# The scan's small products set between the main ones over several halves, and the last projection done for one half of the columns and then for the other

## What is computed

```python
u_a, z_a, b_c, c_c, h_c, z_c, g_a, g_c = jnp.split(x @ w_in, SPLIT_POINTS, axis=-1)
y_a, hr, hi = ssm_branch(u_a, ...)   # 64 groups: complex diagonal scan of 64 states, then GELU and a GLU
y_a = (y_a * jax.nn.silu(z_a)) @ w_out_a
y_c = (b_c * conv3(c_c * h_c) * jax.nn.silu(z_c)) @ w_out_c
merged = jax.nn.sigmoid(g_a) * y_a + jax.nn.sigmoid(g_c) * y_c
r = DN_ALPHA * x + merged @ w_o
rc = r - mean(r); out = rc * rsqrt(mean(rc * rc) + eps) * ln_g + ln_b
```

## Time and profile before

| | |
|---|---|
| median of 3 runs | 1627.57 us (1622.84 to 1632.72) |
| profiled execution, its own time | 1623.52 us |
| its span | 1621.7 us |
| PE busy | 97% of the span |
| granted TensorE clock, mean | 0.976 of full |

### The profile page before, as it was taken

How to read it: one execution, slowest core, us unless ns; L and a number is a source line. 1 busy time by engine, 2 the same in 40 slices (tenths; PEclk the granted TensorE clock), 3 DMA queues, 4 the chain that set the end, 5 groups by cost and what they waited for, 6 DMA issues and landing times.

```text
span 1621.7 us, 26870 instructions
## 1 busy us (share of the span) xinstructions
PE 1570.0 (97%) x11852; PEld 1565.4 (97%) x11852; DVE 769.2 (47%) x1014; ACT 402.2 (25%) x498; POOL 188.4 (12%) x348
## 2 busy tenths in 40 slices
PE   8999999999999999999999999999999999999990
PEld 8999999999999999999999999999999999999990
DVE  5976373464463552632523533223733455343438
ACT  4222222222122222222222122223421222221214
POOL 0110031121211211311213112010000000000000
PEclk9999999999999999999999999999999999999995
DMA  8352262452443534634625434254544343232312
GB/s 304 108 154 91 89 170 73 115 144 88 125 119 95 154 98 122 171 109 124 165 75 164 123 115 140 88 157 140 174 156 134 126 139 115 93 110 91 125 46 116
DMA packets 78084, 204.42 MB, mean 126 GB/s; under 512 B 18704, under 2 KB 19216, under 8 KB 77968
## 3 DMA queue, kind: packets, MB, share of 16 engines
q1 hardware_dynamic: 62096, 172.00, 33.2%
q0 software_dynamic: 15872, 30.70, 8.0%
HBM read 169.77 MB, written 28.16 MB: 122 GB/s over the span
## 4 chain that ended last, share of the span: by engine, by line
PE 92%; DVE 5%; SPq 1%; issue 0%; DMA 0%; ACT 0%; DVEq 0%
PE acc L582 87%; DVE r_all L1369 1%; DVE w_lo L881 1%; DVE r_all L1368 1%; SPq L385 1%; PE y_ps L626 0%; PE y_ps L627 0%; PE y_ps L625 0%; PE y_ps L624 0%; DMA w_raw<-in_w 0%; PE y_ps L623 0%; PE v_ps L603 0%; PE v_ps L602 0%; PE y_ps L622 0%; PE v_ps L601 0%
## 5 line engine op out<-in xcount | busy, mean ns | idle before, releaser
L582 PE MATMUL acc<-xh,w_hi 128*128 128x288 f32 x2560 | 557.0, 299 | 11.1 <-DVE w_lo L881 11.1
L582 PE MATMUL acc<-xl,w_hi 128*128 128x288 f32 x2560 | 554.9, 298 | 0.0
L582 PE MATMUL acc<-xh,w_lo 128*128 128x288 f32 x2560 | 554.8, 298 | 0.0
L881 DVE TENSOR_TENSOR w_lo<-w_raw,w_hi 128x1024 fp32r<-128x1024 f32 x232 | 283.8, 1224 | 441.8 <-ACT w_hi L692 440.4
L582 PEld LDWEIGHTS acc<-xh,w_hi 128*128 128x128 f32 x2560 | 416.6, 191 | 13.1 <-DVE w_lo L881 7.4
L582 PEld LDWEIGHTS acc<-xh,w_lo 128*128 128x128 f32 x2560 | 416.9, 191 | 0.0
L582 PEld LDWEIGHTS acc<-xl,w_hi 128*128 128x128 f32 x2560 | 416.4, 191 | 0.0
L692 ACT ACTIVATE w_hi<-w_raw 128x1024 fp32r<-128x1024 f32 x232 | 245.3, 1057 | 645.0 <-PE acc L582 629.4
L582 PE MATMUL acc<-mh,w_hi 128*128 128x288 f32 x512 | 110.1, 296 | 0.0
L582 PE MATMUL acc<-mh,w_lo 128*128 128x288 f32 x512 | 109.9, 295 | 0.0
L582 PE MATMUL acc<-ml,w_hi 128*128 128x288 f32 x512 | 109.9, 295 | 0.0
(11 more groups left out here) (266 smaller groups left out, 1501.0 us busy)
## 6 DMA issues: line engine op xcount, KB each, us to landing
w_raw<-in_w SPq DMA_DIRECT2D x232, 512.0 KB, 3.7
sg_dram<-out_st SPq DMA_DIRECT2D x32, 288.0 KB, 4.5
v_sw<-v_st POOLq DMA_DIRECT2D x32, 144.0 KB, 4.9
gc_in<-sg_dram SPq DMA_DIRECT2D x16, 288.0 KB, 2.8
sz_in<-sg_dram SPq DMA_DIRECT2D x16, 288.0 KB, 2.8
x_in<-in_xT SPq DMA_DIRECT2D x16, 288.0 KB, 2.8
outT<-o_st SPq DMA_DIRECT2D x16, 288.0 KB, 2.1
mb<-mq_dram POOLq DMA_DIRECT2D x8, 512.0 KB, 6.6
```

Of the source, the lines that this page charges most:

```text
L582: ins = pe.matmul(acc[:, par, t, 0:TH], w, m[:, k0 + k, t * TH:(t + 1) * TH], start=first and k == 0 and n == 0, stop=last and k == KH - 1 ...
L881: dve.tensor_tensor(w_lo[h % NW][:, :], w_raw[:, h % NW, :], w_hi[h % NW][:, :].bitcast(F32), ALU.subtract).then_inc(lo_ready, 1)
```

## The change

**In the scan.** `states_in`, `taps` and `outputs` no longer stand ahead of a half. They are emitted inside `half`, one product at a time behind a pair of main products, at the 24 places (`at`) of a half: `states_in` over halves 9 and 10 (one small product at every second place), the taps in half 10 (one at every third place), `outputs` over halves 19, 20 and 21 (at two of three places). The steps of the other engines move with them. On ACT lch, lbh and uh all come in step 7 (they were in 3 and 4), DVE's lbl and ul in step 8 (5), and so on; POOL fetches the next block's matrices ahead of `load_lt`, not behind it. The loads of `y_in` ahead of the GLU go two at a time, and their last `yl` comes in loop 157 instead of 159.

**In the last projection** all 32 halves are done for the columns t = 0 (24 main products each), and then all 32 again for t = 1, so the weights are loaded and split twice. The sums, the variance, the norm and the stores for t = 0 run beside the halves for t = 1. `norm_at(q)` spreads the 16 tiles' norms over the halves 38 to 60 of the 64. What is left behind the last half is done for 288 columns.

```diff
+O_PER = 2 * KX
+H_END = H_O + 2 * O_PER
...
-            if (b := ssm_step(h, 9)) is not None:
+            if (b := ssm_step(h, 12)) is not None:
                 pool.wait_ge(v_ready, b + 1)
                 swap(v_sw, v_st, v_swapped)
-            if (b := ssm_step(h, 12)) is not None:
+            if (b := ssm_step(h, 13)) is not None:
                 pool.wait_ge(s_ready, b + 1)
                 swap(v_sw, v_st, s_swapped)
-            if (b := ssm_step(h, 11)) is not None:
+            if (b := ssm_step(h, 14)) is not None:
                 store_k(b)
-            if (b := ssm_step(h, 13)) is not None:
+            if (b := ssm_step(h, 15)) is not None:
                 load_lt(b)
...
-                    for t in range(2):
+                    for t in ts:
                         ins = pe.matmul(acc[:, par, t, 0:TH], w, m[:, k0 + k, t * TH:(t + 1) * TH],
...
+                    for emit, b, part in beside:
+                        emit(b, part, 3 * k + n)
...
+        def states_in(b, part, at):
+            if part == 0 and at == 0:
+                pe.wait_ge(lbl_ready, b + 1)
+                pe.wait_ge(ul_ready, b + 1)
...
+        def taps(b, part, at):
...
+            if at % 3:
+                return
+            g = at // 3
+            x, q = divmod(g, 4)
+            ins = pe.matmul(y_ps[32 * q:32 * q + 32, 0, x * P:(x + 1) * P], bbar[:, g, :],
...
+            beside = [(emit, b, part) for emit, off, part in ((states_in, 9, 0), (states_in, 10, 1), (taps, 10, 0),
+                                                              (outputs, 19, 0), (outputs, 20, 1), (outputs, 21, 2))
+                      if (b := ssm_step(h, off)) is not None]
...
+            if t and u == 2:
+                sums(0)
+            half(h, h % 2, mh, ml, (u // 2) % 2 * KH, u % 4 < 2, u % 4 >= 2,
+                 merged_there if h in (H_O, H_O + 2) else None, ts=(t,))
+        sums(1)
...
-            if (b := ssm_step(h, 3)) is not None:
+            if (b := ssm_step(h, 7)) is not None:
                 act.wait_ge(lc_ready, b + 1)
...
-            if (b := ssm_step(h, 4)) is not None:
                 act.wait_ge(lb_ready, b + 1)
...
+            if (b := ssm_step(h, 8)) is not None:
+                dve.wait_ge(lbh_ready, b + 1)
```

More of the change, by code:

```diff
@@ L330, in build @@
     ml_ready = sem("ml_ready")
-    xin_loaded = [sem(f"xin_loaded{i}") for i in range(2)]
+    xin_loaded = [sem(f"xin_loaded{i}") for i in range(4)]
     r_ready = sem("r_ready")
@@ L344, in build @@
     out_ready = sem("out_ready")
-    y_out = [sem(f"y_out{i}") for i in range(4)]
+    y_out = [sem(f"y_out{i}") for i in range(8)]
     small_stored = sem("small_stored")
@@ L570, in fresh, with half @@
             used[par] += 1
-        def half(h, par, mh_, ml_, k0, first, last, per_block=None):
+        def half(h, par, mh_, ml_, k0, first, last, per_block=None, beside=(), ts=(0, 1)):
             pe.wait_ge(lo_ready, h + 1)
@@ L592, in out_of @@
             return ps[:, t, at:at + CH]
[L594 to L623, removed]
-                pe.matmul(o, ltl[:, g, :], uh[:, g, :], start=False, stop=False)
-                pe.matmul(o, ch, hh[:, g, :], start=False, stop=False)
-                pe.matmul(o, ch, hl[:, g, :], start=False, stop=False)
-                ins = pe.matmul(o, cl, hh[:, g, :], start=False, stop=True)
-            ins.then_inc(y_done, 1)
+        def states_in(b, part, at):
+            if part == 0 and at == 0:
+                pe.wait_ge(lbl_ready, b + 1)
+                pe.wait_ge(ul_ready, b + 1)
+                if b:
+                    pe.wait_ge(v_evac, b)
+            if at % 2:
+                return
+            g, m = divmod(12 * part + at // 2, 3)
+            w, u = ((lbh, uh), (lbh, ul), (lbl, uh))[m]
+            ins = pe.matmul(out_of(v_ps, g), w[:, g, :], u[:, g, :], start=m == 0, stop=m == 2)
+            if (g, m) == (NG - 1, 2):
+                ins.then_inc(v_done, 1)
@@ new lines, in outputs @@
+        def outputs(b, part, at):
+            if part == 0 and at == 0:
+                pe.wait_ge(hl_ready, b + 1)
+                pe.wait_ge(lcl_ready, b + 1)
+                pe.wait_ge(lt_loaded, LT_LOAD * (b + 1))
+                pe.wait_ge(k_evac, b + 1)
+            if at % 3 == 2:
+                return
+            g, m = divmod(16 * part + at // 3 * 2 + at % 3, 6)
+            ch, cl = (t[:, g, :, :].rearrange("p t c -> p (t c)") for t in (lch, lcl))
+            w, v = ((lth[:, g, :], uh), (lth[:, g, :], ul), (ltl[:, g, :], uh), (ch, hh), (ch, hl), (cl, hh))[m]
+            ins = pe.matmul(out_of(y_ps, g), w, v[:, g, :], start=m == 0, stop=m == 5)
+            if (g, m) == (NG - 1, 5):
+                ins.then_inc(y_done, 1)
@@ L860, in _ @@
[L860 to L867 removed]
+            q = h - H_O
+            t, u = divmod(q, O_PER)
@@ new lines, in _ @@
+            l, i = u % 4, u // 4
+            if u == 3:
+                act.wait_ge(pivot_sum, t + 1)
+                act.activation(of_half(pivot, t), v_ps[:, t, 0:TH], ACT.Copy, scale=1.0 / P).then_inc(pivot_ready, 1)
+                square(t, 0)
+            if l == 3 or (l == 2 and i):
+                square(t, i * 2 + l - 2)
+            if q == O_PER + 2:
+                mean_of(0)
+            if q == O_PER + 4:
+                root(0)
+            if (n := norm_at(q - 1)) is not None:
+                finish(0, n)
@@ L869, in _ @@
+        mean_of(1)
+        root(1)
+        for n in range(KX):
+            finish(1, n)
     @blk.vector
@@ L1326, in take_r, with take_d @@
             free(n % 2)
[L1328 to L1331 removed]
+        def take_d(t, n):
+            out, ad, aq, q = (of_half(x, t) for x in (r_all[:, n, :], acc_d, acc_q, sq[n % 2]))
+            dve.tensor_tensor(out, out, of_half(pivot, t), ALU.subtract).then_inc(d_ready, 1)
+            dve.wait_ge(d_ready, t * KX + n + 1)
             if n == 0:
[L1333 removed]
+                link(dve.tensor_copy(ad, out))
@@ new lines, in one_over, with norm @@
+        def one_over(t):
+            r_, m_, mr = (of_half(x, t) for x in (rstd, mean, mean_r))
+            dve.wait_ge(std_ready, t + 1)
+            link(dve.reciprocal(r_, r_))
+            dve.tensor_tensor(mr, m_, r_, ALU.mult).then_inc(rstd_ready, 1)
+            dve.wait_ge(rstd_ready, t + 1)
+        def norm(t, n):
+            out = of_half(r_all[:, n, :], t)
+            link(dve.tensor_tensor(out, out, of_half(rstd, t), ALU.mult))
+            dve.tensor_tensor(out, out, of_half(mean_r, t), ALU.subtract).then_inc(norm_ready, 1)
```

271 lines of the change are left out of this document (147 added, 124 removed).

## The result

| | before | changed |
|---|---|---|
| median (lowest to highest) | 1628.52 us (1622.84 to 1632.72) | 1689.01 us (1680.7 to 1706.0) |
| ratio, 95% interval | | 1.0357 (1.0303 to 1.0411) |
| profiled execution, its own time | 1623.52 us | 1706.0 us |
| its span, mean granted clock | 1621.7 us, 0.976 | 1704.2 us, 0.974 |

The changed kernel is slower by 3.6%, outside the range of the prediction. Its profiled execution was one of its slower ones, 17 us above the median, so its waits are somewhat longer than the usual ones.

What follows compares the result with a forecast made beforehand. PE, busy 97% of the span, was taken to set the time. Terms of 29.6 - 13.2 + 5.6 + 2.5 - 3.9 + 6.5 + 1.5 - 15.1 gave +13.5: 1637 us on the profiled execution, 1640 forecast for the median, range 1616 to 1656.

Steps and rivals of the forecast that it cites:

- the one on `lth` and `ltl`: Scan, PE at `outputs`: waits 0.5 us for the tap loads in five blocks, 2.5 more; bounds 0 and 22.
- The case: Rival: tap loads late by 4 us in five blocks, behind the matrices: 17.5 more, 1658; chance 0.13.
- Lone taps: Half 10: each tap alone pays getting in and out, 0.56 us; 29.6 more in 8 blocks.
- The clock: Scan: small products between main ones avoid the low clock at and behind `outputs`, 13.2 us less.
- `ul`: Scan: PE waits 0.7 us a block for `ul`, 5.6 more in all.
- GLU: Ahead of the GLU: the 2.38 idle and 1.5 of low clock behind it go, 3.9 us less.
- the end: Behind the last half: operations on fewer columns take 15.1 us less of the 40.4.
- the last projection's part: Projection in two passes: 1.5 us more for sums and pivot, 15.1 less at the end; 13.6 less forecast.
- The small products at their new places: Scan: each takes 111 ns between main products as in a row, a term of nothing.
- The pace: From the GLU on: without the idle wait, main products take 133.3 ns, not 130.2; 6.5 us more.

Runs made afterwards that it cites:

- e1: The changed kernel with POOL fetching the next block's matrices at step 11, ahead of the first exchange: 1632.79 us, 1.0012 of before.
- e9: e6 with the taps two at a time at four places of half 10 instead of one group of eight: 1612.95 us.
- e10: e6 with the small products of `states_in` and `outputs` each back in one group (halves 9 and 19): 1621.57 us.
- e4: The kernel before with only the last projection's part of the change; scan as before: 1613.14 us, 0.9890 of before.
- e6: e5 with lbh and uh made in ACT's step 6, lbl and ul in DVE's step 7, one step earlier each: 1602.66 us.
- e8: The kernel before with only the next block's matrices fetched ahead of `load_lt`: 1629.20 us, 0.9996 of before.
- e5: The changed kernel with matrices fetched at step 11 and a block's eight taps as one group behind half 10's last place: 1610.52 us.
- e7: The changed kernel with the loads of taps ahead of the next block's matrices in POOL's loop 15: 1655.78 us, 1.0170 of before.

## Why the prediction failed

The direction was right and the size was not: 13.5 us slower were forecast, 60.5 measured.

**The step that failed** is the one on `lth` and `ltl`, put at 2.5 us with an upper bound of 22. Its count of the chain up to the stores was right to 0.2 us. What failed is the sentence "If the matrices, now ahead of them in the queue, hold them up for 4 us, it is 56": the 4 were taken from no row and left out of the sum, although show POOL's issues of before spread over 19.6 us for twenty DMAs of 0.53 to 0.6 each; its timeline of before has it standing for 8.9 of them. The four loads, two of them of 512 KB, cost 11.7 in block 1 and 7 to 14 in the seven blocks that have them (e1 against the changed kernel). By the prediction's own count the loads came 0.5 too late without them, so there was no slack, and by e1 there were some 2 us. The case did stand among the rivals, as 4 us in five blocks with a chance of 0.13; it was 6.0 to 9.5 in seven. The term was put at 2.5 and measured 56.2 with its clock: that alone is more than the whole miss of 47; the other terms together came out better than forecast. The second mistake is in the same step: "In blocks 5 to 7 DVE waits for no half, the scan is some 5 us earlier, and nothing is late." Seven blocks waited, 5 and 6 among them. There the stores came 25.0 and 26.1 us behind the last tap's next main product, against 28.2 in blocks 0 to 3: 2 to 3 us earlier, not 5, and the matrices cost 14 and 13 there. Only block 7, which fetches no next matrices, did not wait. Third, the wait was given no price for the clock: 18.6 us in the profiled execution. The prediction had the clock of 0.94 behind `outputs` from the earlier trace rows and priced it for the groups that went, and priced nothing of the kind for the waits that came.

**Lone taps.** Right that getting in and out is paid (e9), 0.49 instead of 0.56 each: 22 to 25 us more than the groups, forecast 29.6. The 0.54 behind a main pair is nearly what was forecast; the 0.46 behind a small product is what was over-sized.

**The clock.** Nearly right in size. e10 has 18.9 for its groups, but they are not quite those of before. In the chain of before, the seven rows of 192 main products behind `outputs` are 26.62 to 27.55 us where an undisturbed one is 25.66 (e4, block 3), the eighth block has 1.0 more, and `outputs` itself is 6.51, 7.35 and 5.73 instead of 5.28 in three blocks: 14.8 in all, forecast 13.2. That the clock falls because the small products "leave PE thin" was the author's reading, and no run shows it: in e10 PE is busy throughout the group both in block 0, at 0.83, and in block 1, at 1.00. In the changed kernel the new waits gave all of it back.

**`ul`, GLU, the end.** 5.7 for 5.6; the idle wait ahead of the GLU is gone; the last projection's part is worth 16.7 for 13.6, and the whole of DVE's and ACT's doubled splitting was hidden. The small products at their new places cost 111 ns each: in e6 sixteen halves with their 72 and one group of taps are 110.91, and 16 x 6.4 + 72 x 0.111 + 0.78 is 111.2.

**The pace.** The halves from the GLU on are slow in the changed kernel, as the prediction had it:

```profile
1152.21 329.94 PE acc L611 x2474
```

That is 133.4 ns. But the reason was wrong. e8 keeps the idle wait ahead of the GLU and has the slow pace behind it, 133.5 ns, in its chain:

```profile
1122.20 2.38 issue
1124.59 275.45 PE acc L584 x2064
```

So the wait alone doesn't set the pace. What the traces show is this. In the profiled execution of before the clock fell behind that wait, from 1124.3 to 1127.8, and the main products come 130.0 ns apart from 1128.2 on. They also do from 94.0 to 158.8 and from 814.5 to 835.5, which again is right behind a stretch at a clock of 0.50 and lasts until the next small products or sums; e4 has it once in the scan, from 366.6. In e8 and e4 the clock is 1.00 behind the GLU's wait, and the pace is 133.3. But seven other stretches of before are followed by 133.3, and from 49.7 to 85.6 the fast pace comes without one. So a fall of the clock is not enough either; what decides it stays open, and nothing was tried on it. That execution was 5 us under the median, and the prediction most likely counted its pace twice, once as 6.5 and once as 4.1 for the median.

**The sum again**, from measured terms: lone taps +22.3 (e1 - e5), wait for `ul` +7.9 (e5 - e6), clock -18.9 (e10 - e6), last projection and end -16.7 (e4), late loads with their clock +56.2 (changed - e1). That is +50.8 of 60.5. The 9.7 that are left are the distance from e4 to e10, which have the same products in groups and the same last projection. In their profiled executions it is 6.7 us: e10 has the wait of 4.0 in block 4, and its rows of `outputs` and behind are 19.7 above undisturbed ones where those of e4 are 13.2; against that e4 has the 2.4 of idle time ahead of the GLU and 1.5 of low clock early in block 0. So the groups of before cost some 4 us less by the clock than those of e10, and another 4 of the 9.7 is that wait. The last 3 are the difference between these executions and the medians, on different chips.

## What to carry to other kernels

When a step is moved back in a chain of small steps, count its slack to the consumer first, and then everything that now stands ahead of it in each queue that it uses, by the queue's measured issue time from first to last and not by the time of one issue. Price a long wait of the busiest engine above its length: here the low clock in and behind it took another 2.7 us for each wait of 6 to 9.5. The small products in strips of 32 columns were cheapest together (0.45 to 0.47 us for each further change from the full array and back, e5 and e9), those on the full array between the large ones (e10, with 72 of them a block in two groups, is 18.9 us above e6).

## What was not expected of the hardware

- POOL's queue of DMAs stands still for 9.03 us with no semaphore to wait for, behind two broadcasts of 512 KB, and then issues six in 3.16 us.
- 10.2 us at a clock of 0.50 in and behind each wait of 7.2 to 9.5 us, 6.8 in and behind the one of 6.0, which cost 18.6 us in all; behind `outputs` of before it was 3.4, in two blocks 6.8. In e7 the waits of 1.3 us had no such stretch.
- Two paces of the same 288-column products, 130.0 and 133.3 ns, which change within one execution.
- A group of 48 small products lowers the clock in some blocks of one execution and not in others (e10: `outputs` is 6.26 to 10.43 us in blocks 0, 2, 4 and 6 and 5.28 in the others, of which 3 and 7 have the stretch right behind it and 1 and 5 have none).
